# Down-projection weight loads of a routed mixture of experts, moved from the sync engine's queue to the scalar engine's

## The reference

```python
def expert_block(args):
    xblk, e = args
    hdn = jax.nn.silu(xblk @ w_gate[e]) * (xblk @ w_up[e])
    return hdn @ w_down[e]
```

## Time and profile before

| | us |
|---|---|
| median of three runs (2150.14 to 2152.11) | 2151.71 |
| the profiled execution | 2148.52 |
| its span, first to last instruction | 2146.5 |
| PE matmuls busy | 1919.9 (89%) |
| ACT busy | 582.1 (27%) |
| weights of the experts | 384 transfers of 1 MB by SP |
| granted TensorE clock, mean | 0.961 |

### The profile page before, as it was taken

The page is one execution under the profiler, slowest core; times in us unless marked ns, Lnnn a source line. Parts: engine busy times, 40 slices in busy tenths (PEclk is TensorE's granted clock), DMA queues, the critical chain, the costliest instruction groups (busy, mean ns, idle before and its releaser), DMA issues.

```text
span 2146.5 us, 23952 instructions
## 1 busy us (share of the span) xinstructions
PE 1919.9 (89%) x9724; PEld 1204.4 (56%) x9724; DVE 1178.9 (55%) x1808; ACT 582.1 (27%) x875; POOL 394.8 (18%) x301
## 2 busy tenths in 40 slices
PE   3799999999999999899979999899998898898981
PEld 3687877887787877688834443333333333343330
DVE  6676577567567255412356654454455455454558
ACT  4233223224314255511312222212212212212211
POOL 1642233223224222244210000000000000000002
PEclk9899999999999999999969999999999999999995
DMA  5421221122213221343879999999999999999981
GB/s 196 157 79 40 59 60 53 46 60 59 58 41 86 57 61 60 143 123 98 301 265 411 405 403 408 403 406 403 405 413 408 398 408 405 395 411 403 412 349 78
DMA packets 170847, 505.89 MB, mean 236 GB/s; under 512 B 16336, under 2 KB 108624, under 8 KB 117232
## 3 DMA queue, kind: packets, MB, share of 16 engines
q1 hardware_dynamic: 167552, 491.61, 60.3%
q0 software_dynamic: 2608, 8.53, 1.5%
q10 hardware_dynamic: 576, 4.19, 0.5%
HBM read 499.97 MB, written 12.71 MB: 239 GB/s over the span
## 4 chain that ended last, share of the span: by engine, by line
PE 50%; DMA 30%; DVE 14%; ACT 2%; issue 1%; SPq 1%; POOL 1%; DVEq 0%; ACTq 0%
DMA ring<-in_w_up 30%; PE bank L2062 9%; PE bank L1686 8%; PE bank L1688 8%; PE bank L1687 8%; PE bank L2071 3%; PE bank L1817 2%; PE bank L2031 2%; PE bank L1814 2%; PE bank L1806 2%; DVE half L1158 2%; DVE gd_L L1279 1%; DVE att L1336 1%; DVE sc L1331 1%; SPq L577 1%
## 5 line engine op out<-in xcount | busy, mean ns | idle before, releaser
L2062 PE MATMUL bank<-ring,xbT 128*64 128x512 f32 x2048 | 487.2, 619 | 77.5 <-DMA ring<-in_w_up 75.7
L614 POOL TENSOR_TENSOR wlo<-raw,whi 128x512 fp32r<-128x512 f32 x244 | 340.3, 1426 | 616.7 <-ACT whi L725 393.6
L1557 DVE TENSOR_TENSOR r<-r,bank 128x512 f32<-128x512 f32 x512 | 317.9, 681 | 211.8 <-PE bank L2031 211.2
L2062 PEld LDWEIGHTS bank<-ring,xbT 128*64 128x64 f32 x2048 | 155.9, 141 | 362.2 <-issue 360.2
L1686 PE MATMUL bank<-hTh,wlo 128*128 128x512 f32 x720 | 306.2, 425 | 22.0 <-POOL wlo L614 22.0
L1688 PE MATMUL bank<-hTh,whi 128*128 128x512 f32 x720 | 283.5, 394 | 0.0
L1687 PE MATMUL bank<-hTl,whi 128*128 128x512 f32 x720 | 282.6, 393 | 0.0
L1017 ACT ACTIVATE yw<-bank,wts_all 64x512 f32<-64x512 f32 x256 | 174.6, 682 | 253.8 <-PE bank L2071 249.7
L2071 PE MATMUL bank<-ring,hidT 128*64 128x512 f32 x1024 | 229.4, 601 | 0.5 <-ACT hidT L1010 0.5
L661 POOL DMA_INDIRECT xb<-h_scr,idx_tok x32 | 29.7, 928 | 887.6 <-PE bank L2038 873.3
L2031 PE MATMUL bank<-yhl,place 128*128 128x512 f32 x512 | 158.9, 430 | 11.9 <-DVE r L1557 9.1
(11 more groups left out here) (323 smaller groups left out, 2157.3 us busy)
## 6 DMA issues: line engine op xcount, KB each, us to landing
ring<-in_w_gate SPq DMA_DIRECT2D x128, 1024.0 KB, 28.5
ring<-in_w_up SPq DMA_DIRECT2D x128, 1024.0 KB, 28.9
ring<-in_w_down SPq DMA_DIRECT2D x128, 1024.0 KB, 28.0
raw<-in_w_in SPq DMA_DIRECT2D x45, 1024.0 KB, 5.7
raw<-in_w_o SPq DMA_DIRECT2D x16, 1024.0 KB, 5.1
xt<-in_x SPq DMA_DIRECT2D x4, 1024.0 KB, 9.2
h_scr<-xt SPq DMA_DIRECT2D x4, 1024.0 KB, 7.6
r<-h_scr SPq DMA_DIRECT2D x1, 4096.0 KB, 13.2
```

Source lines behind the costliest of these rows:

```text
L614: i = pool.tensor_tensor(wlo[sl][:, part, :], raw[sl][:, :].rearrange("p (k n) -> p k n", k=KD)[:, part, :], whi[sl][:, part, :].bitcast(F ...
L1557: dve.tensor_tensor(v, v, comb_bank(q, tt)[:, :], ALU.add).then_inc(comb_done, 1)
L2062: i = mm(GU[SLOTS * h:SLOTS * (h + 1), :], xT_[:, k, :], w[:, kk * F:(kk + 1) * F], start=k == 0, stop=k == KD - 1)
```

## The change

The four down pieces of every expert from the second on leave SP's list. ACT issues them from its own hardware queue: the first three of expert `t + 1` straight behind the silu of expert `t`, and the fourth behind the `hidT` copy. Each keeps its buffer, its wait on `w_used` and its semaphore. Expert 0's down pieces, and all gate and up pieces, stay with SP. The helper `weight_source` is only moved.

```diff
             for n in range(NPIECE * E):
                 t, i = divmod(n, NPIECE)
+                if t and i >= 8:
+                    continue
                 if n >= RING:
                     sp.wait_ge(w_used, used_when(n - RING))
...
+            def load_down(t, c):
+                n = NPIECE * t + 8 + c
+                act.wait_ge(w_used, used_when(n - RING))
+                act.dma_start(ring[n % RING][:, :], weight_source(t, 8 + c)).then_inc(w_loaded[n % RING], 16)
+
             def block_act(t):
                 act.wait_ge(w_used, 8 * t + 4)
                 W(act, hT_ps, t)
                 act.activation(hid[SLOTS:P, :], GU[0:SLOTS, :], ACT.Silu).then_inc(sg_done, 1)
+                for c in range(3 if t + 1 < E else 0):
+                    load_down(t + 1, c)
                 act.wait_ge(hT_ps, t + 1)
                 act.activation(hidT[:, :, :], HT_PS[:, 0:KF * SLOTS].rearrange("p (c n) -> p c n", c=KF), ACT.Copy).then_inc(hidT_done, 1)
+                if t + 1 < E:
+                    load_down(t + 1, 3)
                 act.wait_ge(w_used, 8 * t + 8)
```

More of the change, by code:

```diff
@@ L482, in build, with weight_source @@
         BD_E, BD_G, BD_GC = 6, 15, 18
+        def weight_source(e, i):
+            if i < 8:
+                src = [gate_v, up_v][i % 2][:, bass.ds(e, 1), 4 * (i // 2):4 * (i // 2) + 4, :]
+                return src.rearrange("p o k f -> p (o k f)")
+            return down_v[:, bass.ds(e, 1), i - 8:i - 7, :].rearrange("p o c n -> p (o c n)")
         block = ctx.enter_context(nc.Block())
```

## The result

| | before | after |
|---|---|---|
| median, us | 2151.14 (2150.14 to 2152.11) | 2168.69 (2166.49 to 2170.22) |
| the profiled execution | 2148.52 | 2169.35 |
| its span | 2146.5 | 2167.4 |

The kernel became slower by 17.5 us, ratio 1.0081 with a 95% interval of 1.0063 to 1.0098. The forecast was 2162 us, 10.5 us more, with a range of 2150 to 2180.

What follows compares the result with a forecast made beforehand. The prediction took the DMA engines' transfers in the expert stage as the bound. Order of landing added 10.5 us, other terms 0: execution 2148.52 to 2159.0, plus 3.2 for the median, 2162 us; own range 2155 to 2170, overall 2150 to 2180.

Steps and rivals of the forecast that it cites:

- The bound: Expert stage: DMA engines always busy and setting the pace, 31.84 us an expert, with PE having 4.0 us to spare.
- Issue time on ACT: Behind the silu: three issues take 1.1 to 2.0 us, hidT comes 0 to 0.65 us late; value 0.
- Later issue: ACT issues D0 some 5.3 us later, D1 and D2 about 0.6 us; needed over 30 us later; value 0.
- Order of landing: End of the expert stage: down pieces overtake, so the last U3 lands last, 9.9 us later; 10.5 us with clock.
- The 0.6 us put on the clock: Last expert: allowance for slower matmuls if PE's clock falls in the stall, 1.5 us more or 0.
- The rate with two deep queues: Middle of the expert stage: engines' rate with both queues deep, not shown by the profile; taken as 0.
- the bound of 16: Expert stage: 16 us cost if interleaving alone lowered the rate by 2.4% over two thirds of 980 us.
- no change: Rival: pieces land nearly in issue order, or the last down pieces still land behind U3; 2152 us, chance 0.14.
- ACT held: Rival: an issue takes ACT 2.14 us, PE starts the down projection 4.6 us late; 2190 us, chance 0.12.
- faster by SP's issues: Rival: SP's issuing is the bound from expert 7 on; 97 us less, 2055 us, chance 0.05.

Runs made afterwards that it cites:

- e3: Changed kernel with all four of ACT's issues behind the hidT copy: 2168.41 us, ratio 1.0077 to the kernel before.
- e4: Changed kernel with ACT's four issues behind the wait for the last down matmul, ahead of yw: 2162.66 us, ratio 1.0060 to the kernel before.
- e10: As e4, but with the down pieces of experts 28 to 31 on SP: 2157.51 us, ratio 1.0029 to the kernel before.
- e6: Changed kernel without the gathers of experts 2 to 31: 2105.32 us, against 2093.27 us for the kernel before without them.
- e11: Changed kernel with each gather held until PE has used the running expert's second pair: 2163.03 us, ratio 1.0050 to the kernel before.
- e1: Changed kernel with only experts 1 to 30's down pieces on ACT, expert 31's on SP: 2166.71 us, ratio 1.0074 to the kernel before.
- e8: Changed kernel with experts 1 to 27's down pieces on ACT, 28 to 31's on SP: 2156.22 us, ratio 1.0028 to the kernel before.
- e9: Changed kernel with experts 1 to 15's down pieces on ACT, 16 to 31's on SP: 2152.75 us, ratio 1.0014 to the kernel before.
- e2: Changed kernel with only expert 31's four down pieces on ACT, all others on SP: 2160.22 us, ratio 1.0045 to the kernel before.

## Why the prediction was right, and where it was short

- *The bound* stood as told: 1.01 of the DMA engines before and after, and PE's spare time an expert large enough to hide everything else. SP's short issues gained nothing.
- *Issue time on ACT, 0:* right, and with more room than worked out, since the issues run beside the silu and not behind it. e3 confirms it.
- *Later issue, 0:* right for the change. It held because expert 1's down pieces still go out before SP's queue runs dry; e4 and e10, which issue them some 10 us later, left the engines idle for 3.9 and more than 6 us there.
- *Order of landing, 10.5 us:* right in mechanism and size. U3 as the last of the 384 pieces costs 9.7 us, and 9.9 were forecast. Alone, order measured 9.7 us (the last expert only; 7.1 by the stages) and 12.1 us (no gathers; 10.2 by the stages). The 0.6 us put on the clock came out as 0 in the changed kernel, whose last 16 matmuls took 3.65 us, and as 1.7 in e6 and e11, where they took 5.35. What I had told badly is where it arises: I called it a loss at the end of the stage. The end is where it shows, but e1 and e8 showed a lateness that stands in every expert and takes several experts in the right order to work off. Down pieces also landed in 17.4 us, not 21.
- *The rate with two deep queues, taken as 0:* this is the term that was mis-sized, and it is more than a third of the loss. By the last landing it measured 6.3 and 7.6 us (two profiles of the changed kernel), and 6.0 us by the medians with the order restored (e8), inside the bound of 16. The row that I took the bound from, 406 GB/s beside gathers against 416 alone, held the right suspicion, a gather, but I read it as a cost of interleaving in general. Two deep queues by themselves cost nothing (421 GB/s in both, last landings 0.4 us apart). The extra is there only with gathers, and over half of it, 4.3 us by the stages and 4.6 by the medians, goes when the gather is moved away from ACT's fresh pieces. Why 3.3 us stay then is open.
- *Sum:* 9.7 us of order and 6.3 or 7.6 of later landing make the 16.0 and 17.3 us of the two stages; the medians gave 16.8 and 17.5. The forecast of 2162 us came within 7 us of 2168.7, inside its own range of 2155 to 2170 but near its end: the order was sized well, and the other term was left out.
- *The rivals:* no change falls by the 17.4 us of landing, ACT held by its 1.30 us for three issues, and faster by SP's issues at 0.33 us, which brought 402 GB/s and not more than 406. How the gather is slowed inside the engines was not tried.

No version of this change beat the kernel before. The nearest was e9, 2.5 us more, with 60 pieces on ACT and the order restored 16 experts before the end. Few pieces on ACT are no help by themselves: e2 had four there and was 9.7 us slower, since they passed urgent ones at the very end.

## What to carry to other kernels

Where transfers set the pace, the order of one queue is a schedule: a second queue gives its pieces a share of their own, and what isn't urgent then overtakes what is. Look at how far ahead of need each stream is before splitting it off, and count the pieces that will pass the urgent ones, times the time of one. A queue that holds its issuer back is no reason to split it as long as the engines are busy; check the share and the rate first. And an experiment that restores the order at the end alone may show nothing, because the consumer is late by then and can only catch up at its own pace.

## What the runs showed of the hardware

- Two deep hardware queues of 1 MB loads moved the same 421 GB/s as one. With one gather of scattered rows an expert in the software queue it was 406 GB/s beside one deep queue and 402 beside two, the gather landing in 8.2 and 9.4 us; with the gather some 18 us later it landed in 8.2 us beside two, at 404 GB/s.
- ACT's issues of transfers ran at the same time as its activation (1524.31 and 1524.32 us), 1.30 us for three.
- SP's issue of an up piece took 2.14 us in a full queue and 0.33 us with a third of the pieces gone, at no gain in time: the long issue was mostly waiting.
